# A hybrid decoder trunk on one core: the gated delta rule's block-diagonal tables in 64 columns per head, with 64x64 products

## What is computed

```python
tril, strict = jnp.tril(ones(64, 64)), jnp.tril(ones(64, 64), k=-1)
decay = jnp.where(tril, jnp.exp(gc[..., :, None] - gc[..., None, :]), 0.0)
L = jnp.where(strict, jnp.einsum('bnhcd,bnhed->bnhce', k * beta[..., None], k) * decay, 0.0)
rhs = jnp.concatenate([v * beta[..., None], kb * jnp.exp(gc)[..., None]], -1)
u, w = split(lax.linalg.triangular_solve(L + jnp.eye(64), rhs, lower=True, unit_diagonal=True))
a_qk = jnp.where(tril, jnp.einsum('bnhcd,bnhed->bnhce', q, k) * decay, 0.0)
def step(state, inp):          # over the 4 chunks
    qd, kd, uu, ww, aqk, gl = inp
    v_new = uu - jnp.einsum('bhcd,bhde->bhce', ww, state)
    o = jnp.einsum('bhcd,bhde->bhce', qd, state) + jnp.einsum('bhce,bhef->bhcf', aqk, v_new)
    state = state * gl[..., None, None] + jnp.einsum('bhcd,bhce->bhde', kd, v_new)
    return state, o
```

## Time and profile before

| | |
|---|---|
| median of 3 runs | 2422.7 us (2421.3 to 2426.72) |
| profiled execution, own time | 2422.64 us |
| its span | 2420.9 us |
| granted clock of TensorE, mean | 0.996 |
| TensorE matmuls busy | 2376.3 us (98%), 13683 records |
| VectorE / ScalarE / GpSimd busy | 1479.2 / 1065.8 / 248.8 us (61%, 44%, 10%) |
| DeltaNet groups: first and last start of Y (L1068) | 1218.1 and 1549.9 us |

### The profile page before, as it was taken

How to read it: one execution, slowest core, us unless ns; L and a number is a source line. 1 busy time by engine, 2 the same in 40 slices (tenths; PEclk the granted TensorE clock), 3 DMA queues, 4 the chain that set the end, 5 groups by cost and what they waited for, 6 DMA issues and landing times.

```text
span 2420.9 us, 35461 instructions
## 1 busy us (share of the span) xinstructions
PE 2376.3 (98%) x13683; PEld 2077.7 (86%) x13689; DVE 1479.2 (61%) x1563; ACT 1065.8 (44%) x1332; POOL 248.8 (10%) x222
## 2 busy tenths in 40 slices
PE   8999989999999999999999999998999999999999
PEld 7898868888888888889999899977888888888887
DVE  6664577546556555567767758565764555555566
ACT  4455444434444444354635436343443443443442
POOL 0151001001001000000032321310100000000000
PEclk9999999999999999999999999999999999999999
DMA  6663546665666566654524325236466566656654
GB/s 237 186 172 119 184 161 189 199 192 190 192 184 197 193 183 192 200 200 140 174 70 139 115 79 166 70 137 203 138 196 194 185 194 195 185 191 228 190 192 139
DMA packets 236672, 417.09 MB, mean 172 GB/s; under 512 B 23761, under 2 KB 46570, under 8 KB 234986
## 3 DMA queue, kind: packets, MB, share of 16 engines
q1 hardware_dynamic: 235162, 410.73, 53.6%
q10 hardware_dynamic: 1360, 4.19, 0.4%
HBM read 412.77 MB, written 2.10 MB: 171 GB/s over the span
## 4 chain that ended last, share of the span: by engine, by line
PE 83%; issue 10%; DVE 2%; POOL 2%; ACT 1%; DMA 1%; SPq 0%; ACTq 0%; DVEq 0%; POOLq 0%
PE quad L601 20%; PE quad L628 11%; PE quad L630 11%; PE quad L629 11%; PE quad L604 10%; PE quad L572 4%; PE quad L574 4%; PE quad L576 4%; PE quad L1081 1%; PE quad L1068 1%; PE quad L1078 1%; ACT whi L1180 1%; PE quad L670 1%; DMA raw<-in_mem_w_kv 1%; DVE xf L1890 0%
## 5 line engine op out<-in xcount | busy, mean ns | idle before, releaser
L1578 DVE TENSOR_TENSOR wlo<-raw,whi 128x1024 fp32r<-128x1024 f32 x760 | 982.5, 1300 | 704.3 <-ACT whi L1180 701.9
L1180 ACT ACTIVATE whi<-raw 128x1024 fp32r<-128x1024 f32 x760 | 799.7, 1058 | 978.6 <-PE quad L630 506.4
L601 PE MATMUL quad<-xs,whi 128*128 128x512 f32 x2048 | 649.9, 397 | 7.7 <-DVE xs L1898 3.7
L628 PE MATMUL quad<-whi,hh 128*128 128x512 f32 x1248 | 488.6, 392 | 2.1 <-POOL hl L2233 1.3
L630 PE MATMUL quad<-whi,hl 128*128 128x512 f32 x1248 | 485.8, 389 | 0.0
L629 PE MATMUL quad<-wlo,hh 128*128 128x512 f32 x1248 | 485.6, 389 | 0.0
L604 PEld LDWEIGHTS quad<-xs,wlo 128*128 128x128 f32 x2048 | 386.7, 189 | 91.0
L604 PE MATMUL quad<-xs,wlo 128*128 128x256 f32 x2048 | 404.0, 279 | 0.0
L601 PEld LDWEIGHTS quad<-xs,whi 128*128 128x128 f32 x2048 | 314.7, 190 | 10.0 <-issue 5.5
L628 PEld LDWEIGHTS quad<-whi,hh 128*128 128x128 f32 x1248 | 234.3, 188 | 50.4 <-POOL hl L2233 1.7
L630 PEld LDWEIGHTS quad<-whi,hl 128*128 128x128 f32 x1248 | 234.2, 188 | 49.4
(11 more groups left out here) (311 smaller groups left out, 2308.9 us busy)
## 6 DMA issues: line engine op xcount, KB each, us to landing
raw<-in_mlp_w SPq DMA_DIRECT2D x512, 512.0 KB
raw<-in_gdn_w_in SPq DMA_DIRECT2D x105, 512.0 KB
raw<-in_w_out SPq DMA_DIRECT2D x64, 512.0 KB
raw<-in_mem_w_kv SPq DMA_DIRECT2D x32, 512.0 KB
raw<-in_mla_w_in SPq DMA_DIRECT2D x25, 512.0 KB
raw<-in_mla_w_ukv SPq DMA_DIRECT2D x24, 256.0 KB
gb<-in_ln_g SPq DMA_DIRECT2D x4, 1024.0 KB, 7.3
gb<-in_ln_b SPq DMA_DIRECT2D x4, 1024.0 KB, 9.4
```

The lines of the kernel that those rows point to most:

```text
L601: last = nc.tensor.matmul(both, b.whi[:, slot, k, cols], b.xs[:, :, kt, :], start=start, stop=stop, skip_group_check=True)
L628: nc.tensor.matmul(ps[:, t, 0:n], ah[:, kt, toks], hi[:, k, 0:n], start=start, stop=False)
L1180: nc.scalar.activation(b.whi[:, c % NSPLIT], b.raw[:, slot], ACT.Copy).then_inc(sem.hi_ready, 1)
L1578: nc.vector.tensor_tensor(b.wlo[:, c % NSPLIT], b.raw[:, c % NRAW], b.whi[:, c % NSPLIT].bitcast(F32), ALU.subtract).then_inc(sem.lo_ready, 1)
```

## The change

The tables of a chunk are kept compact: 128 partitions (two chunks) by 64 columns per head. The products of the levels become 64x64 matmuls, two for each head: chunk 0 of the tile in rows 0 to 63 and columns 0 to 63 of the array, chunk 1 in rows 64 to 127 and columns 64 to 127 (`blocks`). Level 0 turns `bm` by a matmul with the identity in place of a transpose. The product Z transposed (L1081) is left in the last level only; in levels 2 to 5 `xt` is made by turning `xi` with the identity, after Y and ahead of the weight chunk. VectorE copies it (L2152 of the changed kernel) ahead of the addition. w comes out of 64x128 matmuls into two banks, u out of 64x64 ones. w and q of a chunk lie side by side in `wq`, so that one 128-column weight load and one matmul per head (`wq` by state) take the place of L1100 and L1105; the output of chunks 1 to 3 then lies in the other half of the partitions (`out_half`). The decay table is built from 256 columns in place of 512. Instructions of VectorE, ScalarE and GpSimd on these tables go over 256 columns in place of 512. GpSimd builds the compact masks once. Line numbers of the profile don't hold for the lines with a plus.

```diff
+def out_half(j):
+
+    c = j % 2 if j == 0 else 1 - j % 2
+    return slice(CHUNK * c, CHUNK * (c + 1))
...
+    half = [P, TT, GH, CHUNK]
+    b.bm, _ = at("bm", half, F32, stage)
...
+    b.xi, _ = at("xi", half, F32, o)
...
-    b.qdt, o = at("qdt", quad, F32, o)
-    b.dt, o = at("dt", quad, F32, o)
+    b.wq, o = at("wq", [P, TT, GH, 4, CHUNK], F32, o)
+    b.dt, o = at("dt", half, F32, o)
+    b.tg, _ = at("tg", half, F32, o)
+    b.ntc, _ = at("ntc", half, F32, o)
...
+            def chunk_bank(j):
+                return (side_ps[0], turn_ps[0], side_ps[1], side_ps[0])[j]
...
+            def blocks(f, bank, then):
+
+                for h in range(GH):
+                    for c in range(2):
+                        r = slice(CHUNK * c, CHUNK * (c + 1))
+                        last = f(h, r, bank[r, h * CHUNK:(h + 1) * CHUNK], h == 0)
                 last.then_inc(then, 1)
...
-                    nc.tensor.matmul(side_ps[t][:, :], b.ones[:, :], b.tg[:, t].rearrange("p h c -> p (h c)"),
+                    nc.tensor.matmul(side_ps[t][:, 0:GH * CHUNK], b.blk[:, :], b.tg[:, t].rearrange("p h c -> p (h c)"),
                                      start=True, stop=False, skip_group_check=True)
-                    for h in range(GH):
-                        last = nc.tensor.matmul(side_ps[t][:, h * P:(h + 1) * P], b.identb[:, :], b.negtri[:, :],
-                                                start=False, stop=h == GH - 1, skip_group_check=True)
-                    last.then_inc(sem.p_gb, 1)
+                    nc.tensor.matmul(side_ps[t][:, 0:GH * CHUNK].rearrange("p (h c) -> p h c", h=GH), b.identb[:, :],
+                                     b.negtric[:, :].unsqueeze(1).to_broadcast((P, GH, CHUNK)),
+                                     start=False, stop=True, skip_group_check=True).then_inc(sem.p_gb, 1)
...
-                            each(lambda h, o, s_: nc.tensor.transpose(o, b.bm[:, t, h, :], b.ident[:, :]),
-                                 turn_ps[t], sem.p_y)
+                            blocks(lambda h, r, o, s_: nc.tensor.matmul(o, b.bm[r, t, h, :], b.ident[r, r], start=s_, stop=True, skip_group_check=True),
+                                   turn_ps[t], sem.p_y)
                         else:
                             pe.wait_ge(sem.d_x, (g * (LEVELS - 1) + l - 1) * TT + t + 1)
-                            each(lambda h, o, s_: nc.tensor.matmul(o, b.bm[:, t, h, :], b.xi[:, t, h, :], start=s_,
-                                                                   stop=True, skip_group_check=True),
-                                 turn_ps[t], sem.p_y)
+                            blocks(lambda h, r, o, s_: nc.tensor.matmul(o, b.bm[r, t, h, :], b.xi[r, t, h, :], start=s_,
+                                                                        stop=True, skip_group_check=True),
+                                   turn_ps[t], sem.p_y)
+                    if l > 1:
+                        for t in tiles:
+                            blocks(lambda h, r, o, s_: nc.tensor.matmul(o, b.xi[r, t, h, :], b.ident[r, r], start=s_, stop=True, skip_group_check=True),
+                                   side_ps[t], sem.p_xt)
                     beside(g, 6 + l)
...
                         if l < LEVELS - 1:
-                            each(lambda h, o, s_: nc.tensor.matmul(o, b.xt[:, t, h, :], b.ys[:, t, h, :], start=s_,
-                                                                   stop=True, skip_group_check=True),
-                                 turn_ps[t], sem.p_z)
-                        each(lambda h, o, s_: nc.tensor.matmul(o, b.ys[:, t, h, :], b.xt[:, t, h, :], start=s_,
-                                                               stop=True, skip_group_check=True),
-                             side_ps[t], sem.p_zt)
+                            blocks(lambda h, r, o, s_: nc.tensor.matmul(o, b.xt[r, t, h, :], b.ys[r, t, h, :], start=s_,
+                                                                        stop=True, skip_group_check=True),
+                                   turn_ps[t], sem.p_z)
+                        else:
+                            blocks(lambda h, r, o, s_: nc.tensor.matmul(o, b.ys[r, t, h, :], b.xt[r, t, h, :], start=s_,
+                                                                        stop=True, skip_group_check=True),
+                                   side_ps[t], sem.p_zt)
...
+                    for h in range(GH):
+                        for c in range(2):
+                            r = slice(CHUNK * c, CHUNK * (c + 1))
+                            last = nc.tensor.matmul(turn_ps[c][:, (t * GH + h) * CHUNK:(t * GH + h + 1) * CHUNK], b.kb[r, t, h, :],
+                                                    b.xt[r, t, h, :], start=t == 0 and h == 0, stop=True, skip_group_check=True)
+                    last.then_inc(sem.p_w, 1)
+                    for h in range(GH):
+                        for c in range(2):
+                            r = slice(CHUNK * c, CHUNK * (c + 1))
+                            last = nc.tensor.matmul(side_ps[t][r, h * P:(h + 1) * P], b.xt[r, t, h, :], b.vr[r, t, h, :],
+                                                    start=h == 0, stop=True, skip_group_check=True)
+                    last.then_inc(sem.p_u, 1)
...
+                    ro = out_half(j)
                     m = g * NC + j
                     state = b.st[:, j % 2]
+                    bank = chunk_bank(j)
                     if j:
                         pe.wait_ge(sem.d_s, g * (NC - 1) + j)
-                        each(lambda h, o, s_: nc.tensor.matmul(o[r, :], b.wt[:, t, h, r], state[:, h, :], start=s_,
-                                                               stop=True, skip_group_check=True), turn_ps[0], sem.p_vn)
                         if j == 2:
                             pe.wait_ge(sem.d_u, n0 + 2)
-                        for h in range(GH):
-                            nc.tensor.matmul(side_ps[t][r, h * P:(h + 1) * P], b.qdt[:, t, h, r], state[:, h, :],
-                                             start=h == 0, stop=False, skip_group_check=True)
+                        if j == NC - 1:
+                            pe.wait_ge(sem.a_o, g * NC + 1)
+                        each(lambda h, o, s_: nc.tensor.matmul(o, b.wq[:, t, h, 2 * c:2 * c + 2, :].rearrange("p a i -> p (a i)"),
+                                                               state[:, h, :], start=s_, stop=False, skip_group_check=True),
+                             bank, sem.p_vn)
                         beside(g, 6 + LEVELS - 1 + j)
                     pe.wait_ge(sem.d_vn, m + 1)
                     if j < NC - 1:
...
                                                                skip_group_check=True), turn_ps[1], sem.p_ds)
                     if j == 0:
                         pe.wait_ge(sem.d_u, n0 + 1)
-                    each(lambda h, o, s_: nc.tensor.matmul(o[r, :], b.aq[r, t, h, r], b.vn[r, 0, h, :],
+                    each(lambda h, o, s_: nc.tensor.matmul(o[ro, :], b.aq[r, t, h, :], b.vn[r, 0, h, :],
                                                            start=j == 0 and s_, stop=True, skip_group_check=True),
-                         side_ps[t], sem.p_o)
+                         bank, sem.p_o)
...
+                        nc.scalar.activation(b.ys[:, t].rearrange("p h c -> p (h c)"), turn_ps[t][:, 0:GH * CHUNK],
+                                             ACT.Copy).then_inc(sem.a_y, 1)
...
-                    bank_out(b.wt, t, turn_ps, sem.a_w, scale=-1.0)
+                act.wait_ge(sem.p_w, n0 + TT)
+                for c in range(2):
+                    nc.scalar.activation(b.wq[:, :, :, 3 * c, :], turn_ps[c][:, :].rearrange("p (t h i) -> p t h i", t=TT, h=GH),
+                                         ACT.Copy, scale=-1.0).then_inc(sem.a_w, 1)
...
+                    if l > 1:
+                        for t in range(TT):
+                            dve.wait_ge(sem.p_xt, (g * (LEVELS - 2) + l - 2) * TT + t + 1)
+                            nc.vector.tensor_copy(b.xt[:, t].rearrange("p h c -> p (h c)"),
+                                                  side_ps[t][:, 0:GH * CHUNK]).then_inc(sem.d_xt, 1)
                     for t in range(TT):
-                        m = (g * LEVELS + l) * TT + t
                         if l < LEVELS - 1:
                             dve.wait_ge(sem.p_z, (g * (LEVELS - 2) + l - 1) * TT + t + 1)
                             x_ = b.xi[:, t].rearrange("p h c -> p (h c)")
-                            nc.vector.tensor_tensor(x_, turn_ps[t][:, :], x_, ALU.add).then_inc(sem.d_x, 1)
-                        dve.wait_ge(sem.p_zt, (g * (LEVELS - 1) + l - 1) * TT + t + 1)
-                        x_ = b.xt[:, t].rearrange("p h c -> p (h c)")
-                        nc.vector.tensor_tensor(x_, side_ps[t][:, :], x_, ALU.add).then_inc(sem.d_xt, 1)
```

(37 more changed lines are left out.)

47 lines of the change are left out of this document (25 added, 22 removed).

## The result

The changed kernel took 2385.78 us (median of 4 runs, 2384.13 to 2386.09) against 2423.24 us before on the same chip: a ratio of 0.9844, 95% interval 0.9829 to 0.986. The profiled execution took 2385.69 us, its span is 2384.0. The forecast was 2387.

What follows compares the result with a forecast made beforehand. TensorE's instruction row was taken to bound the kernel. Terms 11.6 + 0 + 2.6 + 1.1 - 2.4 - 1.7 + 0.8 gave 12.0 us per group, 36 in three, from 2422.64 to 2387 us; range 2376 to 2434.

Steps and rivals of the forecast that it cites:

- The shrunken products: Level products as 544 small records per group, two corners side by side at 0.032 us each: 11.6 us gained; chance 0.50.
- B: Rival: TensorE's sequencer sets the pace, about 0.050 us per small record though corners overlap; 2412 us in all, chance 0.20.
- C: Rival: one bank, weight path or strict order keeps the corners apart, 0.057 us per record; 2433 us, chance 0.17.
- D: Rival: a float32 record has a floor, or corner changes drain the array, 0.110 us per record; 2519 us, chance 0.08.
- E: Rival: TensorE's granted clock falls to 1.2 GHz in a quarter of the stretches; 2427 us, chance 0.05 together with others.
- w and u: Products w and u: 16 + 16 records become 32 + 32, side by side, so 0; one after another 3.5 us lost.
- Chunk steps: Eight full-size records replace the 16 of L1100 and L1105 in each of three steps: 2.6 us gained per group.
- Decay table: Table built from 256 columns: 0.57 us less per tile, 1.1 us gained per group for two tiles.
- step 7: Shorter ScalarE, VectorE and GpSimd instructions and the `xt` copies are not on the path, since those engines have idle time.
- Changes of division: Sixteen more changes of the array's division per group at 0.15 us each: 2.4 us lost.
- Waits: TensorE waits ahead of Y, 0.2 to 0.3 us in four levels, ahead of w and for L1149: 1.7 us lost per group.
- The wait at level 1: Level 1's first Y waited for VectorE's identity addition over 512 columns; over 256 it is on time: 0.8 us gained per group.

Runs made afterwards that it cites:

- the run of sixteen: Turns of `xi` alone reordered to 16 records in one corner, then 16 in the other, against the changed kernel; 2393.63 us, 0.9878 of the kernel before.

## Why the prediction was right

1. *The shrunken products.* Right in mechanism, and the size nearly so: 0.0295 to 0.030 us per record against 0.032, thus 12.8 us per group in place of 11.6. Rivals B (0.050), C (0.057) and D (0.110) are out by this number, and E by the stage's clock of 1.00. Of the 0.004 us that the prediction put on top of 0.028, 1 to 2 ns were needed. One premise was not so: 64 of the 544 records, L and q by k, share all rows of the array, and ran side by side all the same.
2. *w and u.* Side by side, 0: right.
3. *Chunk steps.* 0.97 us each, of which 0.12 is the spared change; forecast were 0.87 and 0.15.
4. *Decay table: a step that failed, though the total came out.* From the first record to the weight chunk it took 2.20 us before (1495.20 to 1497.40) and takes 1.01 now (1467.64 to 1468.65): 1.2 gained. But the prediction put the waits behind it at nothing: its step 7 calls the other engines idle by the earlier trace rows, whose stretch begins only behind this place. Late was the scaling of q on VectorE, 0.65 us in each group. Only about 0.5 us was left, and the run with the scaling first got the rest back.
5. *Changes of division.* 0.115 us each, not 0.15: 1.8 to 1.9 us per group in place of 2.4.
6. *Waits.* 0.35 us ahead of Y in four levels where 0.2 to 0.3 had been said, 0.1 ahead of w with its change, 0.28 ahead of the state update: 1.8 us per group, 1.7 forecast. The wait at level 1 went as forecast: from its Y at 1485.92 to Z at 1489.95 there are 4.03 us, which 32 records, a chunk of 12 matmuls (2.76) and two changes fill.

The sum with the measured terms is 12.8 + 2.6 + 0.5 - 1.9 - 1.8 + 0.8 = 13.0 per group; the first two groups show 13.15. Three of them are 39, the medians differ by 37.5, and the two profiled spans by 36.9. The traces show where the spans lose and gain. At the first turn of the keys the changed kernel is 1.3 us ahead already (1192.0 against 1193.3), before the stage begins; why is open. At the first weight matmul of the cross-attention, before and after, it is 40.7 ahead, so the stage gave 39.4:

```profile
1587.01 0.58 PE L628 MATMUL quad<-whi,hh 128*128 128x512 f32 x1
1546.32 0.94 PE L642 MATMUL quad<-whi,hh 128*128 128x512 f32 x1
```

There the changed kernel ran for some us at the lower clock (the third number from the end again), where the kernel before had 1.00:

```profile
1540.00:1560.00 20.00, 17.77 (x90) 15.01 (x89) 14.13 (x21) 7.45 (x16) 3.74 (x2) 0.91 0.31 100
```

0.09 of 20 us is 1.8 us. Just before it TensorE stands still in both kernels, for 2.4 us before and 2.2 after. The second profile of the changed kernel shows 0.91 there as well, but several of the variants above show 1.00 around the same wait of 2.2 us; why it fell is open. Then, in the last MLP, TensorE waits for nothing that the profile names (the view of waits from 1900 to 2100 us, before and after):

```profile
PE quad L601 <- issue: 0.7, 1, 0.7
PE quad L615 <- issue: 2.2, 2, 1.5
```

That is 1.5 us more. The second profile of the changed kernel has only 0.2 us there, so it varies between executions and is no fixed price of the change. 1.3 + 39.4 - 1.8 - 1.5 is 37.4, within 0.5 us of the spans.

That the total lay within 2 us of the forecast is in part luck. Per group, terms 1 and 4 were wrong by 1.2 and -0.6, terms 5 and 6 by 0.5 and -0.1; outside of the stage, the lower clock, the wait and the early lead took 2 us off in all.

## What to carry over

Block-diagonal products can go to different corners of the array, or different halves of its columns, as small matmuls; two at a time then run side by side and the zeros cost nothing. Order the matmuls so that neighbours lie in different places; up to four records in a row in one place cost next to nothing here. When a stage on the bounding engine gets shorter, look through it for each thing that arrived just in time: here three of them took 7 us of what was gained, and two were only a matter of order.

## What the runs showed of the hardware

- Two corners of the array that write the same PSUM bank, in different partitions, run side by side at full rate: 0.0295 us per record against 0.058 for one corner alone (the run of sixteen). As the Trainium skill words the rule that was weighed in the prediction ("TensorEngine Tiling (Array Packing)", section "Gotcha 1: PSUM Pressure"), these two row tiles could not use one bank at the same time; this measurement says that they can when their columns differ too. Row tiles with the same columns and the same bank were not tried: the w products have the same columns, but two banks.
- TensorE starts matmuls out of the program's order, when the place of the array that a later one needs is idle: the interleaved starts of L1092 and L1097, and of w and q, above. The reach seen is three records. The Trainium skill ("TensorE: Matmul & The Clock Gate", section "The mechanism") says that matmuls are strictly in order, in start and end; these starts say otherwise. The order of the ends was not measured.
- Weight loads run side by side too: records of w with 128 columns of weights each at 0.056 us, where one after another took 0.111. A record with 64 columns of weights and 64 moving took 0.058 alone. So 0.111 was not a floor of a float32 record, and the weight load explains it.
- A change of the array's division costs 0.115 us: 0.23 us for two in a level, between the undivided array and 64x64, and 0.12 a step in the run with q and w of a head next to each other.
